# Linear attention's two tiles interleaved step by step, and the softmax heads' first loads and first scores placed earlier, in a hybrid decoder layer

## What is computed

```python
h = rms_norm(x, norm1_gain) * (1.0 + scale1) + shift1
(xa, ya, fq, fk, fv, ff, gq, gk, gv, glow, gg) = jnp.split(h @ w_in, ...)
out_a = rg_lru(conv(xa), ...) * jax.nn.gelu(ya)
out_b = forgetting_attention(fq, fk, fv, ff, fox_b_f, fox_q_gain, fox_k_gain)
out_c = gated_linear_attention(gq, gk, gv, glow, gg, gla_w_alpha, gla_b_alpha, gla_out_gain)
x = x + gate1 * (jnp.concatenate([out_a, out_b, out_c], axis=-1) @ w_out)
h = rms_norm(x, norm2_gain) * (1.0 + scale2) + shift2
gt, up = jnp.split(h @ ffn_w_gate_up, 2, axis=-1)
x = x + gate2 * ((jax.nn.silu(gt) * up) @ ffn_w_down)
```

## Time and profile before

| | us |
|---|---|
| median of 3 runs | 3020.7 (3019.48 to 3022.56) |
| the profiled execution | 3023.98 |
| its span, first to last instruction | 3022.2 |
| PE busy | 2829.3 (94%) |
| DVE busy | 1480.5 (49%) |
| ACT busy | 1189.5 (39%) |
| POOL busy | 1034.6 (34%) |

### The profile page before, as it was taken

The page is one execution under the profiler, slowest core; times in us unless marked ns, Lnnn a source line. Parts: engine busy times, 40 slices in busy tenths (PEclk is TensorE's granted clock), DMA queues, the critical chain, the costliest instruction groups (busy, mean ns, idle before and its releaser), DMA issues.

```text
span 3022.2 us, 32970 instructions
## 1 busy us (share of the span) xinstructions
PE 2829.3 (94%) x12416; PEld 2220.6 (73%) x12416; DVE 1480.5 (49%) x1876; ACT 1189.5 (39%) x1658; POOL 1034.6 (34%) x488
## 2 busy tenths in 40 slices
PE   8999998886889999999999999999999999999999
PEld 4787876565656778887677777877777777878887
DVE  3969785554663434435453445454535554431111
ACT  3333333342343435343442544544435445332222
POOL 2545453311123332234333222333331122444443
PEclk9999999887889999999999999999999999999999
DMA  7555535515535244444623444446244543433332
GB/s 264 178 174 184 168 119 165 164 56 144 177 130 170 67 148 132 134 133 155 199 81 119 130 142 138 143 147 192 81 129 141 149 146 105 156 103 95 98 97 91
DMA packets 159902, 419.05 MB, mean 139 GB/s; under 512 B 18284, under 2 KB 20604, under 8 KB 156672
## 3 DMA queue, kind: packets, MB, share of 16 engines
q1 hardware_dynamic: 157408, 412.48, 43.9%
q10 hardware_dynamic: 2336, 4.46, 0.4%
HBM read 355.95 MB, written 60.92 MB: 138 GB/s over the span
## 4 chain that ended last, share of the span: by engine, by line
PE 61%; DVE 8%; ACT 5%; DMA 3%; issue 3%; SPq 2%; POOL 0%; ACTq 0%; DVEq 0%; POOLq 0%
PE ff_acc_ps L77 16%; PE ff_acc_ps L79 15%; PE ff_acc_ps L78 15%; PE fa_st_ps L1674 2%; PE fa_o_ps L1690 2%; PE fa_s_ps L1648 1%; PE fa_st_ps L1675 1%; DMA ff_w_raw<-in_w_gate_up 1%; PE fa_o_ps L1692 1%; PE fa_s_ps L1649 1%; PE fa_o_ps L1691 1%; DVE ff_silu L1354 1%; SPq L944 1%; PE fa_o_ps L1764 1%; PE fa_st_ps L1727 1%
## 5 line engine op out<-in xcount | busy, mean ns | idle before, releaser
L1076 POOL TENSOR_TENSOR w_lo<-ff_w_raw,w_hi 128x1024 fp32r<-128x1024 f32 (+1 forms) x326 | 770.7, 2365 | 1658.3 <-PE ff_acc_ps L79 1574.4
L77 PE MATMUL ff_acc_ps<-h_odd_hi,w_hi 128*128 128x512 f32 x1856 | 754.0, 406 | 45.0 <-DVE h_odd_lo L1359 13.1
L79 PE MATMUL ff_acc_ps<-h_odd_hi,w_lo 128*128 128x512 f32 x1856 | 739.2, 398 | 0.0
L78 PE MATMUL ff_acc_ps<-h_odd_lo,w_hi 128*128 128x512 f32 x1856 | 738.6, 398 | 0.0
L1091 ACT ACTIVATE w_hi<-ff_w_raw 128x1024 fp32r<-128x1024 f32 (+1 forms) x326 | 338.5, 1038 | 935.4 <-PE ff_acc_ps L79 729.4
L77 PEld LDWEIGHTS ff_acc_ps<-h_odd_hi,w_hi 128*128 128x128 f32 x1856 | 358.5, 193 | 153.2 <-issue 58.1
L79 PEld LDWEIGHTS ff_acc_ps<-h_odd_hi,w_lo 128*128 128x128 f32 x1856 | 357.3, 193 | 78.6
L78 PEld LDWEIGHTS ff_acc_ps<-h_odd_lo,w_hi 128*128 128x128 f32 x1856 | 358.7, 193 | 73.1 <-issue 1.9
L1384 DVE TENSOR_TENSOR fa_p_lo<-fa_probs,fa_p_hi 128x512 fp32r<-128x512 f32 x240 | 152.4, 635 | 295.4 <-ACT fa_p_hi L1125 295.2
L77 PE MATMUL ff_acc_ps<-ff_a_hi,w_hi 128*128 128x512 f32 x704 | 283.3, 402 | 4.0 <-DVE ff_gated L1591 4.0
L78 PE MATMUL ff_acc_ps<-ff_a_lo,w_hi 128*128 128x512 f32 x704 | 279.2, 397 | 0.0
(11 more groups left out here) (262 smaller groups left out, 4089.4 us busy)
## 6 DMA issues: line engine op xcount, KB each, us to landing
ff_w_raw<-in_w_gate_up SPq DMA_DIRECT2D x176, 512.0 KB, 3.8
w_raw<-in_w_in SPq DMA_DIRECT2D x74, 512.0 KB, 4.3
ff_w_raw<-in_w_down SPq DMA_DIRECT2D x64, 512.0 KB, 3.7
mod_w<-in_w_mod SPq DMA_DIRECT2D x24, 1024.0 KB, 5.3
fa_v<-v_split_dram SPq DMA_DIRECT2D x60, 384.0 KB
ff_w_raw<-in_w_out SPq DMA_DIRECT2D x32, 512.0 KB, 4.3
fa_ks_a<-ka_dram SPq DMA_DIRECT2D x60, 256.0 KB
fa_kt_a<-ka_dram SPq DMA_DIRECT2D x60, 256.0 KB
```

The lines of the kernel that those rows point to most:

```text
L77: nc.tensor.matmul(out, hi, act_hi, start=first, stop=False)
L78: nc.tensor.matmul(out, hi, act_lo, start=False, stop=False)
L79: return nc.tensor.matmul(out, lo, act_hi, start=False, stop=last)
L1076: nc.gpsimd.tensor_tensor(w_lo[:, j % LO, wide], w_raw[:, j % RAW, wide], w_hi[:, j % HI, wide].bitcast(F32), ALU.subtract).then_inc(lo_re ...
```

## The change

Five edits. (1) The order of the G steps: steps 0 to 3 of both tiles alternate, then (0,4), (0,5), (0,6), (1,4), (0,7), (1,5), (1,6), (1,7). In block 0 they stand in slots 6 to 12, four of them in slot 6; in blocks 1 to 3 one a slot as before, in the same sixteen slots. (2) z, grow, e_neg, one_e, b_cum and decay get room for both tiles, and waits for the tile before become waits for the block before. (3) The first four scores of block 0 are put into slot 13, the other turns over slots 14 to 22. (4) The region's tiles are laid out anew, so that queries, first keys and `m_cols` lie where linear attention's gk, gv, glow, restart, z and grow lay: their ones wait for the attention products (`att_done`) and not for the stores, in slot 12 in block 0, and the loads of "Q" and "KS" wait for those alone. In block 0 they are issued at the end of slot 10. (5) The ones of `kt_b` and the "KT" loads wait for the stores as before, in slot 14 and ahead of slot 13's `weights`.

```diff
-    A0_AT = G0_AT + GLA_T * G_STEPS // 2 + 1
+    A0_AT = G0_AT + 7 + 1
+
+    G_ORDER = [(j, s) for s in range(4) for j in range(GLA_T)] + [(0, 4), (0, 5), (0, 6), (1, 4), (0, 7), (1, 5), (1, 6), (1, 7)]
+    G0_SLOT = (0, 0, 0, 0, 1, 1, 2, 2, 3, 3, 4, 4, 5, 5, 6, 6)
...
-    for s in range(GLA_T * G_STEPS):
-        side.setdefault(G0_AT + s // 2, []).append([("G", (0, s // G_STEPS, s % G_STEPS))])
-    for x, turn in enumerate(turns_of(0)):
-        side.setdefault(A0_AT + x * (N_PROJ - 1 - A0_AT) // len(turns_of(0)), []).append(turn)
-    x_load, g_load, a_load, fill_at = [0], [G0_AT], [A0_AT - 1], [A0_AT]
+    for at_slot, (j, s) in zip(G0_SLOT, G_ORDER):
+        side.setdefault(G0_AT + at_slot, []).append([("G", (0, j, s))])
+
+    turns = turns_of(0)
+    side[A0_AT - 1] = turns[0:TPB]
+    for x, turn in enumerate(turns[TPB:]):
+        side.setdefault(A0_AT + x * (N_PROJ - 1 - A0_AT) // len(turns[TPB:]), []).append(turn)
+    x_load, g_load, a_load, fill_at, q_fill = [0], [G0_AT], [A0_AT - 1], [A0_AT], [G0_AT + 6]
...
-        for j in range(GLA_T):
-            for s in range(G_STEPS):
-                side[lo + G_STEPS * j + s] = [[("G", (b, j, s))]]
+        for x, (j, s) in enumerate(G_ORDER):
+            side[lo + x] = [[("G", (b, j, s))]]
         lo += GLA_T * G_STEPS + 1
         a_load.append(lo)
         fill_at.append(lo)
+        q_fill.append(lo)
...
             refill(("T", last_item(U - 2)), ("Q", U))
+        elif b == 0:
+            refill(("G", (0, GLA_T - 1, 4)), ("Q", U))
         else:
             put(a_load[b], ("Q", U))
...
-            put(a_load[HEADS[U][0]], ("KS", n))
+            if HEADS[U][0] == 0:
+                refill(("G", (0, GLA_T - 1, 4)), ("KS", n))
+            else:
+                put(a_load[HEADS[U][0]], ("KS", n))
             put(a_load[HEADS[U][0]], ("KT", n))
...
-            gk, gq, gv, gg = (there("ga_" + n, [P, GLA_T, BLK]) for n in ("gk", "gq", "gv", "gg"))
+
+            gk, gv = (there("ga_" + n, [P, GLA_T, BLK]) for n in ("gk", "gv"))
             glow, restart = there("ga_glow", [GLA_RANK, BLK]), there("ga_restart", [P, BLK])
-            z, e_neg, one_e, b_cum, grow = (there("ga_" + n, [P, BLK]) for n in ("z", "e_neg", "one_e", "b_cum", "grow"))
+            z, grow, e_neg, one_e, b_cum, gq, gg = (there("ga_" + n, [P, GLA_T, BLK]) for n in ("z", "grow", "e_neg", "one_e", "b_cum", "gq", "gg"))
...
-                        sp.wait_ge(filled, 3 * (b + 1))
+                        sp.wait_ge(filled, 3 * b + 2)
                         sp.dma_start(q_a[:, n % 2].bitcast(F32), q_split[h, :, cols(b)]).then_inc(q_in[n % 2], 16)
...
-                        sp.wait_ge(filled, 3 * (HEADS[U][0] + 1))
+                        sp.wait_ge(att_done, 2 * GLA_T * (HEADS[U][0] + 1))
                         sp.dma_start(ks_a[:, n % 2].bitcast(F32), ka[h, :, cols(c)]).then_inc(ks_in[n % 2], 16)
...
-                def ones(b):
-                    pool.wait_ge(g_out, 16 * GLA_T * (b + 1))
+                def ones_for_queries(b):
+                    pool.wait_ge(att_done, 2 * GLA_T * (b + 1))
                     nc.gpsimd.memset(q_b[HEAD_DIM:].bitcast(F32), 1.0).then_inc(filled, 1)
                     pool.wait_ge(filled, 3 * b + 1)
+                    nc.gpsimd.memset(m_cols[:].rearrange("p a t r -> p (a t r)").bitcast(F32), 1.0).then_inc(filled, 1)
+                    pool.wait_ge(filled, 3 * b + 2)
+
+                def ones_for_keys(b):
+                    pool.wait_ge(g_out, 16 * GLA_T * (b + 1))
                     nc.gpsimd.memset(kt_b[HEAD_DIM:].bitcast(F32), 1.0).then_inc(filled, 1)
-                    pool.wait_ge(filled, 3 * b + 2)
-                    nc.gpsimd.memset(m_cols[:].rearrange("p a t r -> p (a t r)").bitcast(F32), 1.0).then_inc(filled, 1)
                     pool.wait_ge(filled, 3 * b + 3)
...
+                        if j == q_fill[b]:
+                            ones_for_queries(b)
                         if j == fill_at[b]:
-                            ones(b)
+                            ones_for_keys(b)
...
                     if s == 2:
                         act.wait_ge(cumulated, 5 * i + 5)
-                        if i >= 1:
-                            act.wait_ge(state_done, 2 * NCH * i)
-                        nc.scalar.activation(z[:], one_e[:], ACT.Exp, scale=1.0 / GLA_TAU).then_inc(grown, 1)
+                        if b >= 1:
+                            act.wait_ge(state_done, 2 * NCH * GLA_T * b)
+                        nc.scalar.activation(z[:, j], one_e[:, j], ACT.Exp, scale=1.0 / GLA_TAU).then_inc(grown, 1)
...
-                        nc.vector.tensor_tensor_scan(b_cum[:], restart[:], e_neg[:], 0.0, ALU.mult, ALU.add).then_inc(cumulated, 1)
+                        nc.vector.tensor_tensor_scan(b_cum[:, j], restart[:], e_neg[:, j], 0.0, ALU.mult, ALU.add).then_inc(cumulated, 1)
```

More of the change, by code:

```diff
@@ L1060, in prepare @@
                     for b in range(NBLK):
-                        if j >= GIVEN and j in (x_load[b], g_load[b], fill_at[b]):
+                        if j >= GIVEN and j in (x_load[b], g_load[b], q_fill[b], fill_at[b]):
                             pool.wait_ge(lo_ready, split(j))
@@ L1195, in linear @@
-                        nc.scalar.activation(decay[:], chunks(b_cum[:])[:, :, GLA_CHUNK - 1], ACT.Exp, scale=1.0 / GLA_TAU).then_inc(grown, 1)
+                        if b >= 1:
+                            act.wait_ge(state_done, 2 * NCH * GLA_T * b)
+                        nc.scalar.activation(z[:, j], one_e[:, j], ACT.Exp, scale=1.0 / GLA_TAU).then_inc(grown, 1)
+                        nc.scalar.activation(grow[:, j], b_cum[:, j], ACT.Exp, scale=-1.0 / GLA_TAU).then_inc(grown, 1)
+                        nc.scalar.activation(e_neg[:, j], b_cum[:, j], ACT.Exp, scale=1.0 / GLA_TAU).then_inc(grown, 1)
@@ L1196, in linear @@
+                        nc.scalar.activation(decay[:, j], chunks(b_cum[:, j])[:, :, GLA_CHUNK - 1], ACT.Exp, scale=1.0 / GLA_TAU).then_inc(grown, 1)
                     if s == 3:
@@ L1504, in linear @@
                                     dve.wait_ge(state_done, 2 * NCH * i + 2 * c + h - 1)
-                                nc.vector.scalar_tensor_tensor(out=state[half(h), c + 1, half(h)], in0=state[half(h), c, half(h)], scalar=decay[half(h), c:c + 1],
+                                nc.vector.scalar_tensor_tensor(out=state[half(h), c + 1, half(h)], in0=state[half(h), c, half(h)], scalar=decay[half(h), j, c:c + 1],
                                                                in1=st_ps[half(h), c % 2, (c // 2) * P + HEAD_DIM * h:(c // 2) * P + HEAD_DIM * (h + 1)],
@@ L1741, in linear @@
                             pe.wait_ge(state_done, 2 * NCH * i)
-                        for w, src in ((0, gv[:, j]), (1, k_end[:])):
+                        for w, src in ((0, gv[:, j]), (1, k_end[:, j])):
                             for t in range(TPB):
@@ L1748, in linear @@
                             for t in range(TPB):
-                                last = nc.tensor.matmul(s_ps[:, bank_of(("att%d" % h, (b, j))), t * P:(t + 1) * P], k_dec[half(h), t * P:(t + 1) * P], q_dec[half(h), t * P:(t + 1) * P], start=True, stop=True)
+                                last = nc.tensor.matmul(s_ps[:, bank_of(("att%d" % h, (b, j))), t * P:(t + 1) * P], k_dec[half(h), j, t * P:(t + 1) * P], q_dec[half(h), j, t * P:(t + 1) * P], start=True, stop=True)
                             last.then_inc(att_done, 1)
@@ L1763, in linear @@
                                 m = 2 * t + c
-                                nc.tensor.matmul(o_ps[:, j, m * GLA_CHUNK:(m + 1) * GLA_CHUNK], state[:, m], q_dec[:, m * GLA_CHUNK:(m + 1) * GLA_CHUNK],
+                                nc.tensor.matmul(o_ps[:, j, m * GLA_CHUNK:(m + 1) * GLA_CHUNK], state[:, m], q_dec[:, j, m * GLA_CHUNK:(m + 1) * GLA_CHUNK],
                                                  start=t == 0 and c == 0, stop=False, skip_group_check=True)
@@ L1771, in linear @@
                         bank_free(("gmean", (b, j)))
-                        nc.tensor.matmul(s_ps[:, bank_of(("gmean", (b, j)))], head_ones[:], squares[:], start=True, stop=True).then_inc(gmean_done, 1)
+                        nc.tensor.matmul(s_ps[:, bank_of(("gmean", (b, j)))], head_ones[:], squares[:, j], start=True, stop=True).then_inc(gmean_done, 1)
                 def gate(t):
```

63 lines of the change are left out of this document (30 added, 33 removed).

## The result

The changed kernel takes 2984.8 us (median of four runs, 2981.9 to 2993.3) against 3021.6 of the kernel before on the same chip (3019.5 to 3023.1): a ratio of 0.9883, 95% interval 0.9867 to 0.9898, 36.8 us less. The forecast was 2980 with a range of 2963 to 3004.

The account below looks back on a forecast made before the run. TensorE works nearly all the time, so only its waits and the half clock behind them can be gained. Gains 7 + 8.6 + 14 + 12 + 2 = 43.6, taken as 41: 3024.0 - 41 - 3.3 = 2980 us, range 2963 to 3004.

Parts of the forecast that it names:

- the eviction's and the state's waits: Block 0: new PE stalls, 3.5 us in slot 9 for slot 7's eviction, some 6.6 in slot 12 for state updates.
- the signs of being wrong: Silu waits over 15 us, weight waits behind early query loads in slots 11 to 13, or first transposed score after 695.
- the wait at the first transposed score: Block 0: the load's wait becomes one of 6 to 8 us, one slot later, behind weight tile and square roots.
- Part 1: Block 0's two linear-attention tiles interleaved in slots 6 to 12, before 6 to 13: gain 7 us (0 to 12).
- Slots 6 and 7 start as before: Block 0: start times unchanged; the second z matmul, Abs and Exp delay the first chain by about 1 us.
- Rival A: Waits replaced: second chain also takes 8.7 us, slot 14's weight wait takes the loads' gain; 2996 to 3007, chance 0.27.
- Parts 2 and 3: Block 0: earlier query and first key loads gain 8.6 us (3 to 12); heads over slots 14 to 22 gain 14 (8 to 18).
- the clock: Fewer waits in block 0 and later leave PE less time at half clock: gain 2 us (0 to 6).
- Part 4: Blocks 1 to 3: earlier loads save 11.6 and 3.7 us, chains in g/u slots cost 3.0 net: gain 12 (4 to 17).
- The rule against it: DVE and GpSimd share ports under an exclusive lock, so every pair of back-to-back chains could take 8.7 us twice.
- B: Nothing gained: memset order and SyncE's in-order queue undo the early loads; within 6 us of 3021, chance 0.04.
- C: Slower: in g/u slots of blocks 1 to 3 ScalarE's exponentials hold the silu; 3028 us and more, chance 0.04.

Follow-up runs that it names:

- after_again: The changed kernel run and profiled once more with no edit: 2983.2 us, ratio 0.987 to the kernel before.
- block0_tile_by_tile: Changed kernel with block 0's linear attention tile by tile over slots 6 to 13, slot 14 empty, turns over slots 15 to 22: 3006.8 us, 0.9956.
- late_loads: As spread_turns, with block 0's query and first key loads back in slot 13 behind the gated output's store: 2998.9 us, 0.9918.
- spread_turns: Changed kernel with block 0's four first scores out of slot 13, all turns spread over slots 14 to 22: 2996.7 us, 0.9913.
- reciprocals_earlier: Changed kernel with the recurrence's rates and its three one-less-decay reciprocals one slot earlier: 2987.9 us, 0.9903.
- queries_wait: Changed kernel with query memsets, and so query and key loads, of blocks 1 to 3 waiting for the gated outputs' stores again: 2992.9 us, 0.9902.
- tile_by_tile: Changed kernel with linear attention of blocks 1 to 3 tile by tile again, block 0 still interleaved: 2973.6 us, 0.9839.
- keys_behind: Changed kernel with key-transposed and value loads of the first two chunks in blocks 1 to 3 put behind the weight tiles: 2975.5 us, 0.9842.
- both: Changed kernel with the edits of keys_behind and tile_by_tile together: 2969.2 us, 0.9819.
- all_three: As both, with block 0's key-transposed and value loads also behind weight tiles, and the rates and reciprocals one slot earlier: 2965.1 us, 0.9825.
- two_reciprocals: As both, with block 0's key-transposed and value loads also behind weight tiles, and the third one-less-decay behind the second in slot 12: 2961.6 us, 0.9793.

## Why the prediction was right, and where it was not

**The sum** of 43.6 (41 taken) against 39.8 in after_again's profile: 34.2 at slot 24 for the forecast's 31.6 in block 0, and 5.6 for its 12 in blocks 1 to 3. Of the 34.2, 2.0 were there at the start of slot 6, ahead of everything that the change touches; the parts below make the other 32.4. Of the signs named, the eviction's and the state's waits, slot 24 and the turned maxima came as said, no weight tile kept PE in slots 11 to 13, and none of the signs of being wrong appeared; the key's wait did not go from blocks 1 to 3, and the wait at the first transposed score was 0.92, not 6 to 8.

**Part 1, block 0's linear attention (gain 7).** From slot 6 to the start of slot 13 after_again takes 92.0 us; before, slot 6 to slot 14 took 102.2 (678.38 less 576.21). Less the 5.44 of the slot not yet done the gain is 4.8. The mechanism is as told: the second chain runs beside an idle GpSimd and took 4.1 us (608.68 to 612.79), the eviction held slot 9 for 3.40 (forecast 3.5), the state held slot 12 for 4.2 (6.6). The step that failed is "Slots 6 and 7 start as before": slot 6, with the second z matmul pair, takes 24.8 us instead of 19.0, of which 2.0 are a longer wait for the gates (9.90 for 7.87). In block0_tile_by_tile slot 6 takes 20.7 with a wait of 9.1, so about 4 of the 5.8 belong to the interleaving. Rival A's lock did not catch this chain, as forecast.

**Parts 2 and 3 and the clock (8.6, 14, 2).** From there to slot 24 the gain is 27.6 (145.2 less 123.0, plus 5.44) for a forecast of 24.6. The split into two parts was wrong: late_loads shows block 0's loads worth 2 without the early scores (5.3 by slots 13 to 23), spread_turns the early scores worth 13 (7.6 by those slots). "So the load's wait turns into a wait of 6 to 8 us one slot later, at the first transposed score" was wrong by place: the wait for weights and square roots exists (6.95 in spread_turns, 6.44 in reciprocals_earlier), but in the changed kernel PE comes to it late, because slot 13 has already waited 4.97 for a maximum behind VectorE's reciprocal and slot 14 2.2 for another. 4.97 + 2.2 + 0.92 are 8.1, so the sum came out by a replacement that I had not seen; that the two sizes agree is luck. My list of what VectorE has ahead of the maxima named the scans of slots 16 to 18 and not the reciprocal of slot 13. The last five maxima cost 7.2 instead of 4.5 (5.3 and 4.1 of the trace less slot 14's 2.2), and slot 24's wait fell by 2.7 (forecast 2).

**Part 4, blocks 1 to 3 (gain 12).** The 5.6 are not the change's alone. The time from slot 24 to the end, by stretches of slots in us, one profile each:

| slots | before | changed, first profile | after_again | queries_wait | tile_by_tile |
|---|---|---|---|---|---|
| 24 to 37, not touched | 117.0 | 119.8 | 120.0 | 117.1 | 120.2 |
| linear attention: 38 to 53, 117 to 132, 193 to 208 | 338.3 | 339.4 | 341.1 | 339.7 | 330.0 |
| up to the first heads: 54 to 63, 133 to 139, 209 to 215 | 188.4 | 183.0 | 175.7 | 187.3 | 178.0 |
| the rest | 1555.0 | 1555.1 | 1556.3 | 1554.9 | 1556.5 |

In the two rows that the change touches after_again gains 9.9 and the first profile 4.3; 4.3 and 2.9 are lost in the others, most of it in slots 24 to 37, where queries_wait, the same kernel there, takes as little as the kernel before. Of silu's growth from 8.4 to 12.8 in after_again 2.7 come there too (4.2 for 1.5). Why such a stretch varies by 3 us no run shows.

The mis-sized step is the loads: "The waits, 21.6 - 10.0 = 11.6 in all, go, with 3.7 of the silu's 8.4" makes 15.3. But 3.7 and 5.9 us of key waits remain in the two profiles, and silu waits stay in the head slots (5.5 in after_again, 3.8 before); the third row is shorter by 12.7 and by 5.4, and taking the early loads back costs 10 to 12. A weight tile stood behind the key-transposed loads, and keys_behind gets 7.8 of it. The order, "I count 3.1 in each block, 9.3, less the waits of that kind and of the decays that go, 6.3", makes 3.0, and against the kernel before the second row shows 2.8 and 1.1. The three waits are 3.10, 3.07 and 3.07, as forecast; two of them bring 1.7 of half clock each, and block 1's was there before the change too (3.1 in the earlier trace rows). In exchange block 2's wait of 2.6 for the decays is gone: its sixteen slots take 113.3 us for 115.9, and block 3's 113.3 for 109.4. The 9.6 of tile_by_tile are more because its slots are also faster than those of the kernel before: its block 2 has no wait for the decays and takes 108.5, while both, with the same order, has that wait of 2.6 and takes 111.4. What decides whether that wait appears is open.

**The rule against it.** The Trainium skill (SBUF — State Buffer, Who interferes with whom) has the pair of ports as an exclusive lock. Block 0's second chain escaped it; in blocks 2 and 3 it is part of the wait: 2.72 us for an operation of 0.69, beside a subtraction of 3.05. The trace agrees.

**Rivals.** B and C are out. A had the lock in the wrong block, and slot 14's wait for weights took nothing; it gave 14 to 25, and the measured gain is 37.

## What to carry over

A wait that is removed is a gain only up to what is late next, and in an in-order queue that is whatever stands behind it: read the queue of each engine at the place where the wait ends, and ask whose queue the moved work now stands in: a chain of five VectorE operations cost PE nothing in a u or d slot, and a wait of 3.1 us in a g slot, where a silu stands behind it. Two waits in a row may each look worthless when taken away alone (slot 13's maximum, slot 14's square roots) and be worth 4 to 8 us together (all_three and two_reciprocals against both). And take a second profile before explaining a few us in one, and compare the stretches that the edit does not touch first: two slots with the same waits took 25.9 and 32.7 us.
